# Hybrid decoder block: order and homes of transfers in the sample attention and the mixing stage

## What is computed

```python
h = rms_norm(x, norm1_g) * (1 + sc1) + sh1
q, k, v, u = split(h @ w_in)                    # 8 heads x 64; u is 2 x 512
# three dilated windows (128,1), (512,4), (2048,16), merged by their softmax denominators
o_attn = combine_dilations([dilated(q, k, v, w, d) for w, d in patterns])
glu = u[..., :512] * sigmoid(u[..., 512:])
dw = causal_depthwise_conv(glu, conv_dw, width=31) + conv_dw_b
o_conv = silu(layer_norm(dw, conv_ln_g, conv_ln_b)) @ w_pw2
x = x + g1 * (concat(o_attn, o_conv) @ w_o)
h2 = rms_norm(x, norm2_g) * (1 + sc2) + sh2
x = x + g2 * (relu(h2 @ w_ff1) ** 2 @ w_ff2)
```

## Time and profile before

| | |
|---|---|
| median of 3 executions | 2694.7 us (2694.52 to 2695.51) |
| the profiled execution's own time | 2694.16 us |
| its span | 2692.4 us |
| busy share: TensorE, VectorE, ScalarE, GpSimd | 95%, 64%, 45%, 42% |
| mean granted TensorE clock | 0.981 |

### The profile page before, as it was taken

One profiled execution on the slowest core, in us unless ns is written; L12 is line 12 of the kernel. 1 busy time (PEld: TensorE's weight loads), 2 busy tenths in 40 slices (PEclk: granted clock), 3 DMA queues, 4 the chain that ended last, 5 costly groups with the idle time before them and its releaser, 6 DMA issues.

```text
span 2692.4 us, 45827 instructions
## 1 busy us (share of the span) xinstructions
PE 2568.0 (95%) x16346; PEld 2276.3 (85%) x16346; DVE 1719.6 (64%) x3928; ACT 1216.3 (45%) x3051; POOL 1134.6 (42%) x795
## 2 busy tenths in 40 slices
PE   6999989999999869998899999999999999999998
PEld 3778757877777537886899999999999999999998
DVE  3268889988999447875655555555555555555555
ACT  4343423558888324554444333434433343443332
POOL 0000000008997035563555444545544453555553
PEclk8999999999999989998999999999999999999999
DMA  7767525844444974663324432452444235245222
GB/s 290 280 208 241 195 105 202 271 129 120 140 139 155 363 271 146 225 201 108 126 89 166 141 136 95 139 166 88 148 165 137 96 124 170 94 136 178 79 63 83
DMA packets 310864, 431.25 MB, mean 160 GB/s; under 512 B 19450, under 2 KB 239590, under 8 KB 304102
## 3 DMA queue, kind: packets, MB, share of 16 engines
q1 hardware_dynamic: 287946, 378.49, 42.1%
q0 software_dynamic: 5088, 39.58, 4.1%
q10 hardware_dynamic: 17604, 10.24, 1.3%
HBM read 353.72 MB, written 146.65 MB: 186 GB/s over the span
## 4 chain that ended last, share of the span: by engine, by line
PE 44%; issue 2%; DVE 2%; DMA 2%; POOL 1%; ACT 1%; SPq 1%; DVEq 0%; POOLq 0%; ACTq 0%
PE ff_u_ps L3219 15%; PE ff_u_ps L3221 15%; PE ff_u_ps L3220 14%; DMA gluT<-h_d 1%; POOL ff_w_lo L2864 1%; DMA out_y_prompt_dram<-ff_x_own 0%; SPq L2782 0%; DVE ff_wT L3076 0%; POOL ff_h_lo L2873 0%; ACT ff_h_hi L2921 0%; DMA ff_x_own<-x_d 0%; PE ff_out_ps L3214 0%; DVE ff_x_own L3101 0%; ACT ff_w_hi L2912 0%; DVE ff_wT L3038 0%
## 5 line engine op out<-in xcount | busy, mean ns | idle before, releaser
L2864 POOL TENSOR_TENSOR ff_w_lo<-gluT,ff_w_hi 128x512 fp32r<-128x512 f32 x342 | 458.0, 1346 | 406.8 <-ACT ff_w_hi L2912 406.7
L3219 PE MATMUL ff_u_ps<-ff_a_hi,ff_w_hi 128*128 128x352 f32 (+1 forms) x1536 | 492.6, 321 | 10.7 <-POOL ff_a_lo L2879 9.2
L3220 PE MATMUL ff_u_ps<-ff_a_lo,ff_w_hi 128*128 128x352 f32 (+1 forms) x1536 | 492.5, 321 | 0.0
L3221 PE MATMUL ff_u_ps<-ff_a_hi,ff_w_lo 128*128 128x352 f32 (+1 forms) x1536 | 492.3, 321 | 0.0
L3219 PE MATMUL ff_u_ps<-ff_h_hi,ff_w_hi 128*128 128x352 f32 (+1 forms) x1368 | 441.6, 323 | 14.4 <-DVE ff_h_lo L3024 5.8
L3221 PE MATMUL ff_u_ps<-ff_h_hi,ff_w_lo 128*128 128x352 f32 (+1 forms) x1368 | 439.2, 321 | 0.0
L3220 PE MATMUL ff_u_ps<-ff_h_lo,ff_w_hi 128*128 128x352 f32 (+1 forms) x1368 | 437.6, 320 | 0.0
L3119 DVE SCALAR_TENSOR_TENSOR ff_y<-ff_u_ps,modT,ff_y 128x352 f32<-128x352 f32 (+2 forms) x336 | 188.1, 570 | 317.6 <-PE ff_u_ps L3221 317.5
L2864 POOL TENSOR_TENSOR ff_w_lo<-ff_wT,ff_w_hi 128x512 fp32r<-128x512 f32 x168 | 225.4, 1343 | 272.1 <-ACT ff_w_hi L2912 191.2
L2912 ACT ACTIVATE ff_w_hi<-gluT 128x512 fp32r<-128x512 f32 x342 | 211.5, 626 | 273.6 <-PE ff_u_ps L3221 257.7
L3219 PEld LDWEIGHTS ff_u_ps<-ff_a_hi,ff_w_hi 128*128 128x128 f32 x1536 | 289.5, 188 | 13.0 <-POOL ff_a_lo L2879 10.3
(11 more groups left out here) (363 smaller groups left out, 5000.7 us busy)
## 6 DMA issues: line engine op xcount, KB each, us to landing
gluT<-in_w_ff_dram SPq DMA_DIRECT2D x192, 512.0 KB, 4.9
out_new_k_sample_dram<-in_cache_k_dram SPq DMA_DIRECT2D x40, 511.0 KB, 6.1
out_new_v_sample_dram<-in_cache_v_dram SPq DMA_DIRECT2D x40, 511.0 KB, 6.2
dwq<-in_w_ada_dram SPq DMA_DIRECT2D x32, 512.0 KB, 8.8
gluT<-in_cache_k_dram SPq DMA_DIRECT2D x16, 1024.0 KB, 9.7
gluT<-h_d SPq DMA_DIRECT2D x80, 176.0 KB, 4.2
mx_acc<-acc_d SPq DMA_DIRECT2D x16, 768.0 KB, 8.2
out_new_k_sample_dram<-in_cache_k_dram POOLq DMA_DIRECT2D x3, 4088.0 KB, 15.6
```

What stands on the lines that cost most here:

```text
L2864: pool.tensor_tensor(slot_view(w_lo, s), src, slot_view(w_hi, s).bitcast(F32), ALU.subtract).then_inc(w_lod, 1)
L3219: pe.matmul(out, w_hi[:, s % WR, w], hi, start=first, stop=False, skip_group_check=more)
L3220: pe.matmul(out, w_hi[:, s % WR, w], lo, start=False, stop=False, skip_group_check=more)
L3221: return pe.matmul(out, w_lo[:, s % WR, w], hi, start=False, stop=last, skip_group_check=more)
```

## The change

In the sample attention SyncE issues the fifth key load ahead of the store of the third pattern's statistics, and doesn't wait for stores any more before the next loads; VectorE waits for them at its first `lower`. `dwq` is kept until the mixing's end (`late`), and isn't stored. The 25 statistics loads of GpSimd become six of SyncE, behind the first convolution tile: one for pattern 0, four for pattern 1, one for pattern 2, with the same bytes. The two loads of attention outputs move into the mixing's program, behind two rows of w_o, and `acc` is a tensor of the mixing. There, tiles 8 to 15 of the convolution are turned from `dwq` without a load; tile 16 uses slot 0. `w_raw` takes `h2`'s memory and `gate_b` the second half of `x1`.

```diff
--- before.py
+++ after.py
@@ -148,7 +148,6 @@
         sv_in = [whole.enter_context(nc.semaphore(f"sv_in{i}")) for i in range(2)]
         pa_out = [whole.enter_context(nc.semaphore(f"pa_o_out{i}")) for i in range(2)]
         pa_st_out = whole.enter_context(nc.semaphore("pa_st_out"))
-        pa_dw_out = whole.enter_context(nc.semaphore("pa_dw_out"))
         qk_t_out = [whole.enter_context(nc.semaphore(f"qk_t_out{i}")) for i in range(2)]
         os_out, stat_in = whole.enter_context(nc.semaphore("os_out")), whole.enter_context(nc.semaphore("stat_in"))
         acc_in = [whole.enter_context(nc.semaphore(f"acc_in{i}")) for i in range(2)]
@@ -220,10 +219,12 @@
 
         held = ExitStack()
         gluT = held.enter_context(nc.sbuf_tensor("gluT", [P, CC, HIST + SEQ], F32))
+        PIECE = 4 * P
+        LATE = 2 * PIECE
+        late = ExitStack()
+        dwq = late.enter_context(nc.sbuf_tensor("dwq", [P, CC, LATE], F32))
         conv = ExitStack()
         with conv:
-            PIECE = 4 * P
-            LATE = 2 * PIECE
             LATE_OPS = TAPS * CC
             QK_OPS = 84
 
@@ -231,7 +232,6 @@
                 return conv.enter_context(nc.sbuf_tensor(name, shape, dt))
 
             gluS = cv("gluS", [P, CC, DB, HIST + DS])
-            dwq = cv("dwq", [P, CC, LATE])
             both = ExitStack()
             last_hi = both.enter_context(nc.sbuf_tensor("last_hi", [P, 2, KT, P], F32R))
             last_lo = both.enter_context(nc.sbuf_tensor("last_lo", [P, 2, KT, P], F32R))
@@ -1774,7 +1774,6 @@
         lent = ExitStack()
         o_r = lent.enter_context(nc.sbuf_tensor("sa_o_r", [P, 2, DH], F32))
         mx_stat = lent.enter_context(nc.sbuf_tensor("mx_stat", [P, 3, NT, 2, H], F32))
-        mx_acc = lent.enter_context(nc.sbuf_tensor("mx_acc", [P, 2, 3, AW], F32))
         mx_dwt = lent.enter_context(nc.sbuf_tensor("mx_dwt", [P, 2, CC, P], F32))
 
         with ExitStack() as st:
@@ -1847,11 +1846,9 @@
                         load_sample_values(sp, g, j, a, values_at(j, a))
 
                     sp.dma_start(sbias[:].rearrange("p a c -> p (a c)"), sbias_d).then_inc(b_in, 16)
+                    load_k(G)
                     sp.dma_start(st_d[2], stat[:, 2].rearrange("i t s h -> i t (s h)")).then_inc(pa_st_out, 16)
-                    sp.wait_ge(pa_st_out, 16 * 3)
-                    for half in range(2):
-                        sp.wait_ge(pa_out[half], o_stored[half])
-                    for n in range(G, 2 * G):
+                    for n in range(G + 1, 2 * G):
                         load_k(n)
                     load_v(0, 1, 0)
                     load_v(0, 2, 0)
@@ -1859,7 +1856,6 @@
                     load_v(0, 3, 0)
                     sp.dma_start(vnew[:], O["new_v_sample"][0, :, WINC - DS:WINC].rearrange("b t h d -> t b (h d)")).then_inc(n_in, 16)
                     sp.dma_start(mask[:], I["mask_h"]).then_inc(n_in, 16)
-                    sp.dma_start(dw_d[:, :, SEQ - LATE:SEQ], dwq[:]).then_inc(pa_dw_out, 16)
                     for n in range(2 * G + 1, 3 * G + 1):
                         load_k(n)
                     sp.wait_ge(a_pe, 1)
@@ -1874,13 +1870,17 @@
                         load_v(1, j, 0)
                     sp.wait_ge(o_done, 1)
                     store_sample(sp, 0)
-                    sp.wait_ge(pa_dw_out, 16)
                     sp.dma_start(mx_dwt[:, 0], dw_d[:, :, 0:P]).then_inc(dw_in[0], 16)
+                    sp.wait_ge(pa_st_out, 16 * 3)
+                    rows = mx_stat[:].rearrange("p a i s h -> p a i (s h)")
+                    sp.dma_start(rows[:, 0], st_d[0]).then_inc(stat_in, 16)
+                    by_row = st_d[1].rearrange("i r c -> (i r c)").rearrange("(m p e) -> m p e", m=4, p=P)
+                    for m in range(4):
+                        sp.dma_start(rows[:, 1, m:NT:4], by_row[m].rearrange("p (n c) -> p n c", n=NT // 4)).then_inc(stat_in, 16)
+                    sp.dma_start(rows[:, 2], st_d[2].rearrange("i r c -> (i r) c").rearrange("(a p) c -> p a c", p=P)).then_inc(stat_in, 16)
                     sp.wait_ge(k_pe, 8 * DB)
                     sp.dma_start(wp_raw, I["w_pw2"][0].rearrange("(k p) c -> p k c", p=P)).then_inc(wp_in, 16)
                     sp.dma_start(wl_raw, I["w_o"][0, AW:D, :].rearrange("(k p) c -> p k c", p=P)).then_inc(wl_in, 16)
-                    for i in range(2):
-                        sp.dma_start(mx_acc[:, i], acc_d[:, i * P:(i + 1) * P].rearrange("a t c -> t a c")).then_inc(acc_in[i], 16)
                     sp.dma_start(mx_dwt[:, 1], dw_d[:, :, P:2 * P]).then_inc(dw_in[1], 16)
 
                 @block.gpsimd
@@ -1894,17 +1894,6 @@
                             col = DS * (2 * c + hh)
                             ins = pool.tensor_copy(qblk[part, :, c, col:col + DS], qs[part, c, :].rearrange("p (b t) -> p b t", t=DS))
                     ins.then_inc(blk_done, 1)
-                    pool.wait_ge(pa_st_out, 16 * 3)
-                    pool.wait_ge(pa_dw_out, 16)
-                    pool.wait_ge(sv_in[0], 16 * 2 * G)
-                    rows = mx_stat[:].rearrange("p a i s h -> p a i (s h)")
-                    by_row = st_d[2].rearrange("(i k) r c -> k r i c", k=8)
-                    pool.dma_start(rows[:, 0], st_d[0]).then_inc(stat_in, 16)
-                    for k in range(8):
-                        r = k // 2
-                        for m in (2 * k % 4, 2 * k % 4 + 1):
-                            pool.dma_start(rows[r:P:4, 1, m:NT:4], st_d[1, 32 * m:32 * m + 32, 4 * r:4 * r + 4]).then_inc(stat_in, 16)
-                        pool.dma_start(rows[16 * k:16 * k + 16, 2], by_row[k]).then_inc(stat_in, 16)
 
                 @block.tensor
                 def _(pe):
@@ -2003,6 +1992,9 @@
                         v.wait_ge(s_pe, 2 * g + (2 if p == 2 else 1))
                         if g == 0:
                             v.wait_ge(b_in, 16)
+                            v.wait_ge(pa_st_out, 16 * 3)
+                            for half in range(2):
+                                v.wait_ge(pa_out[half], o_stored[half])
                         else:
                             v.wait_ge(p_pe, 3 * g)
                         return v.tensor_tensor_reduce(prob[:, p], s_ps[:, S_OF[p]], sbias[:, p], 1.0, -NEG, ALU.add, ALU.min, mins[:, p:p + 1])
@@ -2038,7 +2030,6 @@
                         v.wait_ge(o_pe, g + 1)
                         if g == 0:
                             v.wait_ge(n_in, 16 * 2)
-                            v.wait_ge(pa_dw_out, 16)
                         step(v.scalar_tensor_tensor(out=o_m[:].rearrange("p (h d) -> p h d", d=DH), in0=o_ps[:].rearrange("p (h d) -> p h d", d=DH),
                                                     scalar=mins[:, 7:8], in1=mask[:].unsqueeze(2).to_broadcast([P, H, DH]), op0=ALU.mult, op1=ALU.mult))
                         v.tensor_reduce(o_r[:, g], o_m[:].rearrange("p (h d) -> p d h", d=DH), AX.X, ALU.add).then_inc(o_done, 1)
@@ -2093,11 +2084,10 @@
 
             wo_hi = sb("wo_hi", [P, KT, D], F32R)
             wo_lo = sb("wo_lo", [P, KT, D], F32R)
-            w_raw = sb("w_raw", [P, 2, D])
             gate_p = sb("gate_p", [P, D])
             gate_s = sb("gate_s", [NS, D])
-            gate_b = sb("gate_b", [P, D])
-            stat, acc, dwt = mx_stat, mx_acc, mx_dwt
+            stat, dwt = mx_stat, mx_dwt
+            acc = sb("acc", [P, 2, 3, AW])
             least = sb("least", [P, NT, H])
             fac = sb("fac", [P, NT, 3, H])
             total = sb("total", [P, NT, H])
@@ -2117,6 +2107,8 @@
             rs2 = sb("rs2", [P, 4])
             x1n = sb("x1n", [P, D])
             h2 = sb("h2", [P, 2, KT, P])
+            w_raw = h2[:].rearrange("p a k t -> p a (k t)")
+            gate_b = x1[:, 1]
             dw_ps = ps("dw_ps", [P, CW])
             y_ps = ps("y_ps", [P, CC, P])
             f_ps = ps("f_ps", [P, 512])
@@ -2139,13 +2131,18 @@
 
             fold_ps = [f_ps, z_ps[0], z_ps[1]]
 
+            def held_conv(i):
+
+                return NT // 2 <= i < NT
+
             with nc.Block() as block:
                 @block.sync
                 def _(sp):
                     def load_conv(i):
                         n = rows_of(i)
-                        if i >= 2:
-                            sp.wait_ge(S["dw_pe"], i - 1)
+                        if held_conv(i):
+                            return
+                        sp.wait_ge(S["dw_pe"], min(i, NT // 2 + 1) - 1)
                         sp.dma_start(dwt[:, i % 2, :, 0:n], dw_d[:, :, i * P:i * P + n]).then_inc(dw_in[i % 2], 16)
 
                     def load_acc(i):
@@ -2153,7 +2150,7 @@
                         t = slice(i * P, i * P + n)
                         if i >= 2:
                             sp.wait_ge(S["o_d"], i - 1)
-                        if 2 <= i < NT:
+                        if i < NT:
                             sp.dma_start(acc[:, i % 2], acc_d[:, t].rearrange("a t c -> t a c")).then_inc(acc_in[i % 2], 16)
```

(14 more changed lines are left out.)

## The result

The changed kernel takes 2680.34 us, the median of 4 executions (2677.85 to 2682.98), beside 2695.11 us of the kernel before (2694.52 to 2697.77): a ratio of 0.9941, interval [0.9927, 0.9954]. The forecast was 2675.6 us and its range 2670.5 to 2683.5. The profiled execution took 2682.67 us (span 2680.8), so the profile accounts for 11.5 us less than before where 19.1 had been forecast. The table cuts both profiles at the same three points: TensorE's first matmul of the sample attention, of the mixing and of the feed-forward part.

The account below looks back on a forecast made before the run. Bounds taken: SyncE's wait for its statistics store and GpSimd's late statistics loads at the stage's end. 2.8 + 1.9 + 11.6 + 1.3 + 1.5 = 19.1 us off 2694.16, plus 0.5, gives 2675.6 us; range 2670.5 to 2683.5.

Parts of the forecast that it names:

- The fifth key load: Sample attention: issued ahead of the statistics store, the key lands at 898.9, behind the bias load; 2.8 us gained.
- so it still falls before 898.9: TensorE's clock, during the fifth key's wait: falls at 897.6, so nothing gained; 3.0 us more if it did not.
- idle engines take the key: Rival, chance 0.12: fifth key lands at 897.3 through empty DMA engines and the clock holds; 1.6 + 3.0 us more, 2671.0.
- The waits behind it: Sample attention: without the 2 MB convolution store, TensorE's waits for a late key and a late value go; 1.9 us.
- The stage's end: Sample attention's end: GpSimd's 25 issues go, and the mixing starts 1.0 us behind VectorE instead of 12.65; 11.6 us.
- dear end: Rival, chance 0.11: the 5.0 us belong to the stage's end, not GpSimd's DMAs; 4.0 and 1.3 us lost, 2680.9.
- I take 2.0: Statistics loads from SyncE: transfer takes 2.0 us of all DMA engines, from GpSimd's 809 packets at 39 ns each.
- the rival: Small pieces, chance 0.15: 64 B pieces not joined, statistics take 10.3 us, w_o lands late; about 6 us lost, 2681.6.
- The start of the mixing: Mixing's first products: come sooner because the transposes before them run at full clock; 1.3 us, bounds 0 and 1.7.
- so it should hold: TensorE's clock at the mixing's start: stays high, since the pause shrinks to 3.0 us and the fall came 4.0 in.
- Eight convolution loads less: Mixing: one removed load stood ahead of the merged outputs, so TensorE loses less time; 1.5 us, bounds 0 and 1.8.
- The merged outputs come 1.6 to 2 us sooner: Mixing: attention outputs that GpSimd waits 9.9 us for arrive sooner once a convolution load of 1.62 us issue goes.

Follow-up runs that it names:

- e1: The kernel before, with only the fifth key load ahead of the statistics store and the store waits on VectorE: stage 94.21 us, median 2691.26 us, ratio 0.9983.
- e4: The kernel before, with the fifth key load ahead and the statistics in six SyncE loads: stage 83.14 us, median 2687.26 us, ratio 0.9963.
- e10: The changed kernel with its six statistics loads issued by GpSimd, second run: stage 83.15 us, median 2683.59 us, ratio 0.9948.
- e3: The kernel before, with the late convolution kept in SBUF and merged outputs loaded in the mixing: stage 91.28 us, median 2692.3 us, ratio 0.9984.
- e5: The changed kernel with its six statistics loads issued by GpSimd instead of SyncE, first run: stage 83.11 us, median 2678.0 us, ratio 0.9941.
- a1: The changed kernel, unaltered, run again: stage 77.64 us, median 2680.3 us, ratio 0.9949.
- a2: The changed kernel, unaltered, run once more: stage 78.05 us, median 2676.06 us, ratio 0.9923.
- e6: The changed kernel with the fifth key load also ahead of the bias load: stage 77.68 us, median 2677.0 us, ratio 0.9931.
- e7: The changed kernel with the fifth key load ahead of the bias load and the ninth ahead of three values: stage 76.32 us, median 2676.55 us, ratio 0.9935.
- e8: The changed kernel with the pattern 2 statistics load issued a second time into an unread spare buffer: stage 79.59 us, median 2677.58 us, ratio 0.9926.
- e9: The changed kernel with the fifth key ahead of the bias load and the ninth ahead of three values, second run: stage 77.11 us, median 2675.95 us, ratio 0.9926.

## Why the prediction was right, and where not

**What bounds the kernel.** Right in both places: SyncE's wait for its store, and the stage's end.

**The fifth key load**, 2.8 us forecast, 4.3 us measured in the landing (15.80 to 11.51 us into the stage), inside the bounds, 2.5 to 4.4. The mark was right: the key landed 2.4 us behind the bias load, where 2.48 had been taken. The term that was off is the bias load's own landing, 9.0 us into the stage and not 10.5: it was issued 0.4 us sooner and took 7.7 us instead of 8.7. (The 0.6 us "for the signal" in the early bound stand in no row.) What failed is the step "so it still falls before 898.9": the clock held, and 1.7 us of transposes and 1.2 us of score products came on top, the 3.0 us that the prediction had priced under a rival. That was luck: the clock had fallen just ahead of the stage, and TensorE came 1.4 us later to a shorter pause. Where it had not (e1, e4, e10), the pauses were 5.61, 4.78 and 4.43 us, and the clock fell as forecast. So "idle engines take the key" had its price right and its cause wrong: the key came behind the bias load, and the DMA engines' share was about 0.9 or more in every microsecond from 893 until it landed.

**The waits behind it**, 1.9 us: both are gone, but 0.67 us for the ninth key and some 0.8 us for a short fall of the clock, from 955 to 958.4, are new. Up to TensorE's last matmul the stage is 7.64 us shorter, against 4.7 forecast.

**The stage's end**, 11.6 us: 11.8 measured. The mixing starts 0.85 us behind VectorE, so the "dear end" rival is wrong for this kernel. But the 5.0 us of the kernel before were real: e1, e3, e5 and e10 show that they belong to GpSimd's loads in flight. The rule of the Trainium skill that the prediction cites (page "DMA: Bandwidth & Descriptors", section "Rules for kernel authors"), that spreading DMAs over engines saves only the sequencer's issue time, misses just this part: with a cheap end the kernel before would have started the mixing at 978.28 + 0.85 = 979.1 and not at 983.25, so 4.1 of the 11.8 us are no issue time.

**The statistics.** The step "if every piece costs a packet's 39 ns" had the right count and the wrong price, "I take 2.0" the wrong count: the pieces are not joined on SyncE. 4,224 packets at 13 ns are 3.5 us. "The row of this very transfer" was no row for it, since it came from the other kind of queue. The Trainium skill's rule of 512 B or more (page "DMA: Bandwidth & Descriptors", section "Specifications") pointed the right way, and the trace agrees as far as some 100 GB/s stand beside 420 in those slices. The damage that the rival foresaw did not come, since w_o still landed 1.3 us ahead of its use. SyncE's time had another shape than forecast: the first five loads held it 14.9 us behind keys and values, which cost nothing, since it had nothing else to issue.

**The start of the mixing**, 1.3 us forecast, nothing gained. The step that failed is "so it should hold": TensorE's pause was 2.80 us, as forecast, and the clock fell. The fold starts 4.87 us after the mixing, before 4.68. In every profile of the change, or of it with another order of loads on SyncE (a1, a2, e6 to e9), it fell, between 0.1 us ahead of the mixing's start and 1.1 us behind it.

**Eight convolution loads less**, 1.5 us forecast. The mixing is 0.62 us shorter, and TensorE's wait of 0.72 us that is gone accounts for it. The step that was mis-sized is "The merged outputs come 1.6 to 2 us sooner". Counted from the mixing's start, SyncE issues them at 160.84 us instead of 161.46, 0.6 sooner: the convolution load of 1.62 us is gone, but the issues of the next stage's activations ahead of them took 7.16 us instead of 6.17. GpSimd's wait is 0.7 us shorter, and TensorE's wait of 1.11 us didn't move. Two costs forecast as nothing were nothing: VectorE's wait for stores and the shared buffers show in no wait.

**The sum.** 20.06 us in the two stages against 19.1, by errors that nearly cancel, which is luck: +1.5 and +2.9 at the key, -1.5 for the two new losses, +0.2 at the stage's end, -1.3 and -0.9 in the mixing. The time itself is 4.7 us above the forecast. Of the four executions two lie at 2678 and two at 2683, and the profiled one is of the latter, with the early 4.85 us and the late 2.4 us that the change has no part in; without them it would be at 2675.4, and without the clock that held at the key some 1.5 to 2.9 us above that (1.5 by e8, 2.9 by the terms above). On the three chips the ratio of the medians lies between 0.992 and 0.995, and the forecast's was 0.9929.

**Faster than both kernels?** e7 is the candidate. Its ratios, 0.9935 and 0.9926, lie within those of the change; no gain is shown.

## What to carry to other kernels

Judge an edit of transfers on a full queue together with what it pushes back: the statistics on SyncE cost the mixing 6 to 7 us until the merged outputs behind them had moved and the 2 MB store was gone. An engine that has transfers in flight at a stage's end can hold the stage for their landing, so the engine that issues the last loads matters, and not only how many. And where whole executions scatter by more than the effect, cut the profile at fixed instructions and compare the pieces.
